# A product-key expert layer in a two-block transformer kernel: gates stored by tile in DRAM, a search over 80 candidates, and 48 sparse dots ahead of the V tiles

## The reference, cut to what matters

```python
s_top, i_top = lax.top_k(s, PEER_TOPK)
cand_s = (s_top[:, :, 0, :, None] + s_top[:, :, 1, None, :]).reshape(...)
cand_i = (i_top[:, :, 0, :, None] * PEER_N_KEYS + i_top[:, :, 1, None, :]).reshape(...)
best_s, best_pos = lax.top_k(cand_s, PEER_TOPK)
experts = jnp.take_along_axis(cand_i, best_pos, axis=-1)
g = jax.nn.softmax(best_s, axis=-1)
act = jax.nn.gelu(jnp.einsum('thkd,td->thk', expert_u[experts], xb))
return jnp.einsum('thk,thkd->td', g * act, expert_v[experts])
```

## Time and profile before

| | |
|---|---|
| median of 3 runs | 2555.86 us (2549.32 to 2556.85) |
| profiled execution, its own time | 2555.25 us |
| its span | 2553.4 us |
| mean granted TensorE clock | 0.992 |
| PE, weight loads, DVE, ACT, POOL busy | 96%, 85%, 61%, 37%, 49% |
| DMA, mean over the span | 202 GB/s, 514.52 MB |

### The profile page before, as it was taken

How to read it: one execution, slowest core, us unless ns; L and a number is a source line. 1 busy time by engine, 2 the same in 40 slices (tenths; PEclk the granted TensorE clock), 3 DMA queues, 4 the chain that set the end, 5 groups by cost and what they waited for, 6 DMA issues and landing times.

```text
span 2553.4 us, 37639 instructions
## 1 busy us (share of the span) xinstructions
PE 2441.1 (96%) x12832; PEld 2165.9 (85%) x12832; DVE 1570.3 (61%) x2744; ACT 942.9 (37%) x1420; POOL 1251.5 (49%) x692
## 2 busy tenths in 40 slices
PE   7999998999999999899999998999999999999998
PEld 4878887899999999888888888898867888888887
DVE  5268333089995899669999998997246414422201
ACT  4463333244444455433333333343334323322222
POOL 3215443456667888645555555554411544444443
PEclk9999999999999999999999999999999999999999
DMA  7238322235555576899999999994311323233232
GB/s 272 70 121 293 135 93 97 91 125 173 173 175 170 192 269 211 297 341 400 398 399 400 400 399 399 399 385 151 97 45 34 115 91 99 91 99 95 94 99 74
DMA packets 251610, 514.52 MB, mean 202 GB/s; under 512 B 117440, under 2 KB 150592, under 8 KB 249728
## 3 DMA queue, kind: packets, MB, share of 16 engines
q1 hardware_dynamic: 194672, 345.82, 40.5%
q0 software_dynamic: 38416, 142.36, 13.9%
q10 hardware_dynamic: 18432, 25.17, 2.7%
HBM read 460.85 MB, written 52.43 MB: 201 GB/s over the span
## 4 chain that ended last, share of the span: by engine, by line
PE 64%; SPq 11%; DMA 8%; issue 7%; DVE 6%; POOL 3%; ACT 1%; DVEq 0%; POOLq 0%; ACTq 0%
PE bank L1244 17%; PE bank L1245 16%; PE bank L1246 16%; DMA GJ<-gate_dram 5%; SPq L497 5%; SPq L586 3%; SPq L587 3%; PE pair L1246 3%; PE pair L1245 3%; PE pair L1244 3%; POOL T L679 3%; DMA act_dram<-actb 1%; DVE YROW L2293 1%; DVE wlo L2233 1%; DVE T L2242 1%
## 5 line engine op out<-in xcount | busy, mean ns | idle before, releaser
L625 POOL TENSOR_TENSOR wlo<-wraw,whi 128x1024 fp32r<-128x1024 f32 x319 | 799.1, 2508 | 867.3 <-ACT whi L749 867.1
L1244 PE MATMUL bank<-HH,whi 128*128 128x512 f32 (+1 forms) x2048 | 748.2, 365 | 23.9 <-ACT actb L950 11.6
L1245 PE MATMUL bank<-HL,whi 128*128 128x512 f32 (+1 forms) x2048 | 744.5, 364 | 0.0
L1246 PE MATMUL bank<-HH,wlo 128*128 128x512 f32 (+1 forms) x2048 | 744.2, 363 | 0.0
L749 ACT ACTIVATE whi<-wraw 128x1024 fp32r<-128x1024 f32 x456 | 481.3, 1057 | 451.7 <-PE bank L1246 214.3
L1244 PEld LDWEIGHTS bank<-HH,whi 128*128 128x128 f32 x2048 | 387.5, 189 | 70.6 <-issue 18.7
L1246 PEld LDWEIGHTS bank<-HH,wlo 128*128 128x128 f32 x2048 | 387.0, 189 | 40.5
L1245 PEld LDWEIGHTS bank<-HL,whi 128*128 128x128 f32 x2048 | 387.3, 189 | 39.8 <-issue 0.5
L705 POOL DMA_INDIRECT VROW<-in_w,which x128 | 214.0, 1672 | 167.4 <-DVE YROW L2293 165.3
L1244 PE MATMUL bank<-WH,whi 128*128 128x384 f32 x512 | 184.8, 361 | 51.0 <-DVE WL L2271 50.9
L698 POOL DMA_INDIRECT T<-in_u_rows,which x128 | 130.1, 1017 | 157.4 <-DVE dots L2242 148.2
(11 more groups left out here) (402 smaller groups left out, 3709.7 us busy)
## 6 DMA issues: line engine op xcount, KB each, us to landing
wraw<-in_w SPq DMA_DIRECT2D x456, 512.0 KB
act_dram<-actb ACTq DMA_DIRECT2D x128, 192.0 KB
gate_dram<-GS SPq DMA_DIRECT2D x6, 4096.0 KB, 14.1
AJ<-act_dram SPq DMA_DIRECT2D x128, 192.0 KB
GJ<-gate_dram SPq DMA_DIRECT2D x128, 192.0 KB
adaw<-in_ada SPq DMA_DIRECT2D x32, 512.0 KB
ada<-in_ada SPq DMA_DIRECT2D x16, 512.0 KB, 14.2
NB<-in_nab POOLq DMA_DIRECT2D x4, 1024.0 KB
```

What stands on the lines that cost most here:

```text
L625: nc.gpsimd.tensor_tensor(wlo[:, slot, :, :].rearrange("p k c -> p (k c)"), wraw[:, slot, :, :].rearrange("p k c -> p (k c)"), whi[:, slot ...
L1244: pe.matmul(out_, ah, bh, start=first, stop=False, **kw)
L1245: pe.matmul(out_, ah, bl, start=False, stop=False, **kw)
L1246: return pe.matmul(out_, al, bh, start=False, stop=last, **kw)
```

## The change

The lead falls to 3 iterations a block (48 tiles) and the tail grows from 12 to 28 tiles; `LEAD` grows from 16 to 48 dots: 42 of them in the tail, two behind each of the last 21 low halves, and 6 at the handover to V. The second search looks at 80 candidates: row 0 with all 16, rows 1 to 7 with 8 each, and column 0 of rows 8 to 15; the position is turned back into two indices by six small instructions. The table of key numbers as floats moves from SBUF to PSUM bank 6. `gate_dram` is laid out by tile, `(128, 128, 384)`: each buffer of gates is stored by four DMAs of 32 tiles, 1 MB each in pieces of 256 bytes, one after each of four w loads, and a tile's gates are loaded in one piece of 1536 bytes a partition. The two one-hot instructions of a group become one, with both windows of the gates in PSUM. The count of `g_out` waited for goes from 16 to 64 a block.

```diff
@@ -60,11 +60,11 @@
-U_LEAD = 4
+U_LEAD = 3
 TD = TB - 1
 U_GATE = 4 * TD
-LEAD = 16
+LEAD = 48
 GATE_IT = TB * U_LEAD + 1
@@ -212,7 +212,7 @@
         tki = a2("tki", [P, 16, 16], U32)
-        tkf = a2("tkf", [P, 16, 16])
+        last = a2("last", [P, 2, NH, 16])
         bv = a2("bv", [P, NH, 16])
@@ -224,7 +224,7 @@
         OI = a2("OI", [P, 8, P], FR)
-        OG = a2("OG", [P, 8, 2, P], FR)
+        OG = a2("OG", [P, 2, 2, 4, P], FR)
         s2.close()
@@ -296,10 +296,12 @@
         bank += [pair[b // 2][:, b % 2, :] for b in range(4)]
+        tkf = bank[6][:, 0:256].rearrange("p (n a) -> p n a", n=16)
+        best = T[:, 0:2, :].rearrange("p a b -> p (a b)")[:, 0:NH * 80].rearrange("p (h c) -> p h c", h=NH)
         act_dram = nc.dram_tensor("act_dram", (P, P, SD), F32).ap()
-        gate_dram = nc.dram_tensor("gate_dram", (2 * TD, P, P, 64), F32).ap()
+        gate_dram = nc.dram_tensor("gate_dram", (P, P, SD), F32).ap()
@@ -557,24 +559,18 @@
-            def store_g(b, buf):
+            def store_g(b, part):
                 sp.wait_ge(g_evac, b * 16 + 16)
-                sp.dma_start(gate_dram[b, :, :, :].rearrange("i j t -> i (j t)"),
-                             GS[:, buf, :, :].rearrange("p j t -> p (j t)")).then_inc(g_out[buf], 16)
-
-            for u in range(16):
-                load_w(gu0 + u, u % R)
-            store_g(0, 0)
-            with sp.Fori(0, TD - 1) as i:
-                for half in range(2):
-                    for u in range(8):
-                        load_w(i * 16 + (gu0 + 16 + 8 * half + u), u % R)
-                    store_g(i * 2 + (1 + half), (1 + half) % 2)
+                j = slice(32 * part, 32 * part + 32)
+                sp.dma_start(gate_dram[j, :, 64 * b:64 * b + 64].rearrange("j i t -> i j t"), GS[:, b % 2, j, :])\
+                    .then_inc(g_out[b % 2], 16)
+
+            for n in range(4 * U_GATE + 8):
+                load_w(gu0 + n, (gu0 + n) % R)
+                if n >= 12 and n % 8 >= 4:
+                    store_g((n - 12) // 8, n % 8 - 4)
             gt0 = gu0 + 4 * U_GATE
-            for u in range(8):
-                load_w(gt0 + u, u % R)
-            store_g(2 * TD - 1, 1)
             with sp.Fori(0, U_TAIL - 2) as i:
@@ -584,12 +580,12 @@
                 sp.dma_start(AJ[:, slot, :], act_dram[j, :, :]).then_inc(ring_in[slot], 16)
-                sp.dma_start(GJ[:, slot, :, :], gate_dram[:, :, j, :].rearrange("b i t -> i b t"))\
+                sp.dma_start(GJ[:, slot, :, :].rearrange("p b t -> p (b t)"), gate_dram[j, :, :])\
                     .then_inc(ring_in[slot], 16)
             for b in range(2):
-                sp.wait_ge(g_out[b], 16 * TD)
+                sp.wait_ge(g_out[b], 64 * TD)
             for u in range(R):
@@ -710,7 +706,7 @@
             for b in range(2):
-                pool.wait_ge(g_out[b], 16 * TD)
+                pool.wait_ge(g_out[b], 64 * TD)
             for k in range(R):
@@ -995,7 +991,7 @@
                                 if b >= 0:
-                                    g_group(i * 32 + b, b, i * 16 if b % 16 == 0 and not first else None)
+                                    g_group(i * 32 + b, b, i * 64 if b % 16 == 0 and not first else None)
                                 else:
@@ -1565,7 +1561,7 @@
                     mm = pe.matmul(bank[4 + 2 * half + e // 2][:, e % 2 * 256:e % 2 * 256 + 256], OI[:, t, :],
-                                   OG[:, t, :, :].rearrange("p w j -> p (w j)"), start=True, stop=True)
+                                   OG[:, half, :, e, :], start=True, stop=True)
                 mm.then_inc(g_done, 1)
@@ -2140,21 +2136,32 @@
+                v.wait_ge(sc_evac, 16)
                 sixteen(lambda n: SSc[:, n, :], lambda n: small[:, n, :], lambda n: tki[:, n, :], 16)
-                nc.vector.tensor_copy(tkf[:, :, :], tki[:, :, :])
+                nc.vector.tensor_copy(tkf, tki[:, :, :])
                 halves = small[:, :, :].rearrange("p (h w) a -> p w h a", w=2)
-                then(nc.vector.tensor_tensor(cand, bc(halves[:, 0], 3, 16), bc(halves[:, 1], 2, 16), ALU.add))
-
-                c2 = cand.rearrange("p h a b -> p h (a b)")
-                sixteen(lambda h: c2[:, h, :], lambda h: bv[:, h, :], lambda h: bp[:, h, :], NH)
-                nc.vector.tensor_scalar(bab[:, 0, :, :], bp[:, :, :], 4, None, ALU.logical_shift_right)
-                nc.vector.tensor_scalar(bab[:, 1, :, :], bp[:, :, :], 15, None, ALU.bitwise_and)
+                one, two = halves[:, 0], halves[:, 1]
+                nc.vector.tensor_tensor(best[:, :, 0:16], bc(one[:, :, 0], 2, 16), two, ALU.add)
+                nc.vector.tensor_tensor(best[:, :, 16:72].rearrange("p h (a b) -> p h a b", b=8), bc(one[:, :, 1:8], 3, 8),
+                                        bc(two[:, :, 0:8], 2, 7), ALU.add)
+                then(nc.vector.tensor_tensor(best[:, :, 72:80], one[:, :, 8:16], bc(two[:, :, 0], 2, 8), ALU.add))
+
+                sixteen(lambda h: best[:, h, :], lambda h: bv[:, h, :], lambda h: bp[:, h, :], NH)
+                nc.vector.tensor_scalar(bab[:, 0, :, :], bp[:, :, :], 3, None, ALU.logical_shift_right)
+                nc.vector.tensor_scalar(bab[:, 1, :, :], bp[:, :, :], 7, None, ALU.bitwise_and)
                 then(nc.vector.tensor_copy(hs[:, 1, :], bv[:, :, 0]))
                 then(nc.vector.tensor_copy(babf[:, :, :, :], bab[:, :, :, :]))
-
-                idx = tkf[:, :, :].rearrange("p (h w) a -> p w h a", w=2)
+                row, place, beyond, wide = babf[:, 0, :, :], babf[:, 1, :, :], last[:, 0, :, :], last[:, 1, :, :]
+                nc.vector.scalar_tensor_tensor(beyond, row, 9.0, place, ALU.is_ge, ALU.mult)
+                then(nc.vector.tensor_scalar(wide, row, 1.0, 8.0, ALU.is_equal, ALU.mult))
+                nc.vector.tensor_tensor(wide, wide, beyond, ALU.subtract)
+                then(nc.vector.scalar_tensor_tensor(row, row, 1.0, beyond, ALU.max, ALU.add))
+                nc.vector.tensor_scalar(row, row, -1.0, None, ALU.add)
+                then(nc.vector.tensor_tensor(place, place, wide, ALU.add))
+
+                idx = tkf.rearrange("p (h w) a -> p w h a", w=2)
                 iota16 = bc(bc(iota[:, 0:16], 1, 16), 1, NH)
@@ -2189,7 +2196,10 @@
                 nc.vector.tensor_copy(bank[3][:, 0:P], ITS[:, bass.ds(i * P, P)])
-                nc.vector.tensor_copy(bank[3][:, P:2 * P], GLT[:, bass.ds(i * P, P)].bitcast(F32)).then_inc(win_in, 1)
+                for w, gates in enumerate((GHT, GLT)):
+                    ins = nc.vector.tensor_copy(bank[3][:, P:3 * P].rearrange("p (n w t) -> p n w t", w=2, t=4)[:, :, w, :],
+                                                gates[:, bass.ds(i * P, P)].bitcast(F32).rearrange("p (n t) -> p n t", t=4))
+                ins.then_inc(win_in, 1)
                 v.wait_ge(win_in, i + 1)
@@ -2200,10 +2210,10 @@
                 v.wait_ge(oj_ready, q + 1)
-                oj = OJ[:, n % 4, :, :]
-                for w, gates in enumerate((bank[2][:, bass.ds(q * 4, 4)], bank[3][:, P + 4 * n:P + 4 * n + 4])):
-                    ins = nc.vector.scalar_tensor_tensor(OG[:, ring, w, :], oj, 0.0, bc(gates, 2, P), ALU.is_equal, ALU.mult)
-                ins.then_inc(og_ready, 1)
+                oj = OJ[:, n % 4, :, :].rearrange("p t j -> p (t j)")
+                nc.vector.scalar_tensor_tensor(OG[:, n % 2, :, :, :].rearrange("p w t j -> p w (t j)"), bc(oj, 1, 2), 0.0,
+                                               bc(bank[3][:, P + 8 * n:P + 8 * n + 8], 2, P), ALU.is_equal, ALU.mult)\
+                    .then_inc(og_ready, 1)
@@ -2253,10 +2263,16 @@
             v.wait_ge(sc_evac, 17)
-            for k in range(LEAD):
-                if k < 4 * U_TAIL - 3:
-                    lo(gt + 3 + k, (gt + 3 + k) % R)
-                dot(k, k % R, u_row0[k % R] + 16 * (k // R + 1))
+            def lead_dots(k, n):
+
+                for k in range(k, k + n):
+                    dot(k, k % R, u_row0[k % R] + 16 * (k // R + 1))
+
+            tail = 4 * U_TAIL - 3
+            for t in range(tail):
+                lo(gt + 3 + t, (gt + 3 + t) % R)
+                if t > tail - 1 - (LEAD - 6) // 2:
+                    lead_dots(2 * (t - tail + (LEAD - 6) // 2), 2)
@@ -2280,6 +2296,7 @@
                 pw_low(u, u)
+                lead_dots(LEAD - 6 + 2 * u, 2)
             nc.vector.memset(YROW[:, :], 0.0)
@@ -2305,9 +2322,9 @@
             first = LEAD // 4
-            for i in range(first):
-                v_steps(i, i % 2, max(1, i))
-            with v.Fori(first // 2, (P - LEAD) // 8) as i:
+            for i in range(2):
+                v_steps(i, i, 1)
+            with v.Fori(1, (P - LEAD) // 8) as i:
                 for half in range(2):
```

## The result

The changed kernel takes 2535.64 us (median of 4 runs, 2530.29 to 2536.73) against 2556.36 for the kernel before (4 runs, 2549.32 to 2558.87): a ratio of 0.9919, 95% interval 0.9895 to 0.9943. It is faster by 20.7 us where 42 were forecast. The direction is right, the time lies inside the range, and half of the gain is missing. In the profiled executions it is 2535.67 against 2555.25, 19.6 us.

The account below looks back on a forecast made before the run. No single engine bounds the whole: PE paces the lead, transfers bound V with DVE close behind. Terms -59 - 3 + 55 + 3 - 24 - 14 = -42 from 2555.25 give 2513 us, range 2488 to 2560.

Parts of the forecast that it names:

- The lead: First U tiles beside the expert search: 48 tiles and a shorter search give -59 us, bounds -66 and -42.
- search hidden: Lower bound of the lead's term, -66 us: the search for the best experts is hidden behind PE's 48 tiles.
- The index product: In the lead's search, line 2161: 2.29 us from PSUM instead of 4375 ns, 16.7 us off, 0 as other end.
- The price of the six small instructions: In the lead's search: six new small instructions per block add 14 us for four blocks, bounds 6 and 34.
- The gate stage: 48 U tiles beside one-hot products: the store parts fit, ACT's stall goes, -3 us, bounds -5 and +80.
- The price of a packet: Gate stage stores: a 256-byte packet costs 14.6 to 19 ns; up to 26.5 ns fits.
- The rival of the small stores: Stores of 256-byte runs bound the gate stage; at 40 ns a packet the time is 2596 us; chance 0.16.
- The tail: 28 U tiles with 42 dots: 7 tiles at 4.16 us, 21 at 4.4, +55 us, bounds +50 and +66.
- The rival of slow rows: Rows fetched too slowly in the tail, 10.5 us per us of landing: 2543 or 2564 us; chance 0.11.
- The handover: Between tail and V: six dots and their rows, mostly covered, +3 us, bounds 0 and +7.
- V: Last stretch: 32 tiles without a dot drop to 4.16 us, -24; 79 with a dot to 4.72, -14.
- The likeliest case: Whole kernel: the forecast itself, 2513 us, alone some 2500 to 2532; chance 0.55.

Follow-up runs that it names:

- one row a tile: Changed kernel with seven store parts, V's first rows fetched earlier, LEAD = 32 and one dot behind each of the tail's 25 low halves: 2512.57 us, ratio 0.9828.
- both repairs: Changed kernel with stores in seven parts behind seven w loads and V's first four rows fetched before U's last eight, LEAD still 48: 2516.8 us, ratio 0.9844.

## Why the prediction was right, and where it was wrong

The forecast had the direction right and the big terms of the lead and of V, and half of its gain was missing. One step failed outright, in the gate stage. In the tail a term was sized too small, and at the handover a wait was overlooked.

**The lead.** Right in its mechanism and 7 us too careful: it came out at its bound of -66, "search hidden". The index product takes 2286 ns from PSUM (2.29 forecast, with no row to show it). The price of the six small instructions was mis-sized: 8.4 us in all four blocks for 14. I took the 2.3 us of the longest instruction of the earlier trace rows into the sum once a block. There was one such case in the four blocks, at the first of them (812 ns as the mean of four), and the convert before them, at 2488 ns in its median before, had a median of 286. The compare was slower (3093 for 2292), and still the search ended at 722.0, when PE was about through (it waited 0.7 us), so hardly any of it stood out. With the operand in SBUF it did, by 21.5 us.

**The gate stage.** The step that failed is "So it fits, the parts hold ACT's stores for under 5 us, and the stall goes: -3". The price of a packet was nearly right (an estimate of 20 ns for its 14.6 to 19), the stall of ACT went, and the stage does have room for the bytes: two experiments bring it to 244 us with the same bytes, one of them with the same packets. What the step left out is what it names a few sentences before: the w loads are behind the parts on SP. It asked whether a block's packets fit into a block's 41 us; the stores stand in half of that time. Issuing a w load behind a part took up to 6.3 us, where a tile takes 5.1, and ACT waited 64.4 us in all for weights. That makes +8.7 for -3. The step was too careful on one side too: without the bunching the stage takes 244 us, not 247. The rival of the small stores was right about the place and wrong about the reason: no price per packet near 26.5 ns was needed.

**The tail.** The mechanism was right and the size off. The step reads "7 to 9.1 us for four rows, 3.5 to 4.6 for two. I take 4.4". The formula holds: landing, plus dot, plus issue. The nine landings on the chain between 1045 and 1131 us take 7.0 to 9.1 us, 8.1 in the mean; with 1.2 for the dot and 0.3 to issue this is 9.6 for two tiles, 4.8 a tile, and 4.81 is measured. The forecast had landings of 5.3 and 7.4 from the earlier trace rows, two rows only, and its 4.4 stands for 7.1. 20 x 0.41 = 8 us. Why the rows took 8.1 us is not shown. The bytes that the pairs add don't explain it: in the trace with V's rows first the same pairs landed in 7.1 us at 411 GB/s, and a tile took 4.37, the forecast's value, where the changed kernel moved 382 GB/s. Over all the traces with pairs the landings on the chain run from 6.4 to 9.5 us, and what sets them from one execution to another stays open. The other 8 us lie at the end: 13.1 us from the last low half to the last activation, with PE busy in 7.34 of them at a granted clock of 0.74 (a mix of its 1.2 and 2.4 GHz levels), while ACT waits for a weight tile behind SP's eight loads. The forecast gave the end a tile like the others. The rival of slow rows (10.5 us for each us of landing) describes the first half of this; it came out at a landing of 8.1, one us over the 7.1.

**The handover.** +7.6 for +3, with +7 as the upper end. The forecast counted bytes and overlooked the order on POOL's queue: V's first rows are behind the last fetches of U, which wait until the dots have freed their buffers, and the first then took 9.6 us to land. The edit that puts them first took 3.9 us off in one pair of traces and 5.2 in another.

**V.** Right to 0.4 us in the sum. Cut at the event, 1534.0, a tile with a dot takes 371.8/79 = 4.71, for the 4.72 taken; the 32 tiles that lost theirs are 198.0 - 64.8 = 133.2 us, 4.16 each, as taken. 399 GB/s was not a cap on bytes: it is 415 with 1536-byte packets, and 399 again with the old layout. The estimate that I gave by the Trainium skill (DMA: Bandwidth & Descriptors, "Why small descriptors are slow") was -8; worked out again from its 12.9 ns it is an estimate nearer -12 (768 packets x 3.1 ns over 16 engines, 79 tiles). The old layout costs 16.4, so the rows were the better guide here. What the Trainium skill says of transfers under 512 B (DMA: Bandwidth & Descriptors, "Specifications"), that the engines read, modify and write, can't be seen in any of these traces; what can be seen is that such packets of a store cost some 20 ns and fit.

The range held the time because it reached toward the slow rows. The likeliest case's own range, 2500 to 2532, missed it by 4. The lead and the stretches outside the six came out 10 us better than forecast and hid a third of the 32 us lost in between. With the order on both queues repaired, and one row a tile, the kernel takes 2512.6 us. That this is the forecast's 2513 is chance: that kernel has 32 dots ahead of V and not 48, a gate stage 3 us under the forecast's and 16 more V tiles with a dot. The 48 dots with both repairs take 2516.8.

## What to carry to other kernels

When a big store is cut into parts that interleave with loads on one queue, count the time over the stretch in which they stand, not over the whole period, and look at what the load behind each part must wait for. Spread the parts over all loads of the period, and make them small. When transfers are prefetched through a ring of few buffers, the rate is buffers over landing plus use. A landing read from two rows is a weak number: here it ran from 6.4 to 9.5 us for the same rows, so put in the range, and ask for a rate that the slow end still allows, as one row a tile does. And moving work from a stage bound by bytes is worth only what the receiving stage has free.

## What the hardware showed unexpectedly

- The same product of 2048 elements takes 4367 to 4375 ns with both inputs in SBUF and 2286 with the table in PSUM. The compare beside it, also of two SBUF inputs, ran at means of 2292 to 3590 ns in different kernels, so it isn't two SBUF inputs alone. What else about the table in SBUF makes the product slow stays open.
- The issue of a 512 KB load on SP's queue took up to 6.3 us in the gate stage behind a store of 4096 pieces of 256 bytes, and 0.4 to 1.3 us behind the first three stores of the same size in pieces of 8 KB. The waiting is in SP's issue, and it holds all that stands behind it.
